# First block of a two-block transformer kernel: queries and keys move to chunks 2 to 4 of the projection, keys are turned first, VectorE turns a quarter of the queries

## The chip, the cores and the metric

The kernel runs on one core of one Trainium2 chip. The metric is the device time of one execution in microseconds (us), the median of several runs.

## The reference

The program computes two blocks on 512 tokens of width 1024. The change lies in the first block, whose part that matters is this:

```python
u  = rms_norm(h, norm_w) * (1 + scale) + shift        # 512 tokens
uc = rms_norm(hc, norm_w) * (1 + scale_c) + shift_c   # 256 context tokens
p = u @ w_in                       # q, k, v, a gate for attention, a | g for the convolution, a gate for it
q, k, v = qk_heads(p, ...)         # 8 query heads, 2 key heads of width 64, each rms-normed
q, k = rope_2d(q, angles), rope_2d(k, angles)
k_c, v_c = kv_heads(uc @ w_in[:, K_LO:V_HI], ...)
attn = softmax(q @ [k_c, k].T / 8) @ [v_c, v] * silu(p[za])     # 768 keys
conv = pointwise(silu(layer_norm(depthwise_conv_31(a * sigmoid(g))))) * silu(p[zc])
h = h + gate * (concat[attn, conv] @ w_out)
```

shift, scale and gate are rows of silu(c) @ w_mod, the "modulation". The second block has its own w_mod_2 (24 groups of 512 columns), and a mixer of two attentions: one of them ("dsa") scores 4 query tiles of 128 rows for each of 8 heads, tile q against (q + 1) * 128 keys.

## The kernel before, in words

**Chunks.** Every weight matrix is read in chunks of 256 columns. SyncE (SP) loads chunk n + 2 once VectorE is done with chunk n (`lo_done`). ScalarE (ACT) rounds it to a high part (`split_high`, L1372), VectorE (DVE) subtracts to get the low part (`split_low`, L1825), and TensorE (PE) multiplies three times, high by high, high by low and low by high. Chunk n uses the PSUM banks `acc` of its parity. In the first block the chunks are in this order: 0 to 3 are the convolution's g, a, g, a (`N_GLU`), 4 and 5 are queries (`N_Q`), 6 is keys and values with the context's (`N_KV`), 7 to 10 the two gates (`N_ZA`, `N_ZC`), 11 and 12 the pointwise product (`N_PW`), 13 to 16 the output (`N_WO`). Products of 0 to 3 and 7 on put channels on partitions (`product`, L843 to L845), those of 4 to 6 put tokens there (`by_token`, L863 to L866).

**The program of each engine** is a list in its own fixed order, and engines meet only at semaphores. The loop `for n in range(N_PW)` stands once in the program of PE, once in ACT's and once in DVE's.

**Modulation groups.** A group g of 512 modulation columns is read in 4 ticks (SP's `load_tick`) after the chunks `ticks_of(n)` names; chunk n carries half of group 4 + n // 2, and chunk 10 all four ticks of group 9. Up to `G_POOL` = 10 PE does the sums as small matmuls (`tick`, L775), ACT copies the row (`copy_group`), PE turns it (`turn_group`, L788) and DVE adds the bias (`group_columns`, L1837). From group 10 on GpSimd (POOL) sums them in place (`sum_tick`, L620, L623, L627), and PE adds the partitions (L782). PE's tick of an even chunk waits for `group_columns` of the group before it. Group columns stand in DVE's list in the middle of its taps.

**Queries and keys.** After chunk 6 ACT squares, DVE reduces, ACT takes the root (`qrs_rd`), DVE norms keys (`kn_rd`), and POOL norms the queries (L559, L561) and applies the rotation: for each of 4 token tiles first the keys (8 operations of 64 columns), then the queries (6 of 256), then it copies the context's keys (L586), and only then raises `rope_rd`. It then clears half of each key buffer (L594), since `kH`, `kL` (kept in the memory of `uH`, `uL`) hold each key head twice, padded with zeros to 128 partitions. PE, past chunk 10, waits for `rope_rd`, turns 4 query blocks (L897) and 2 key blocks (L900) through the banks `X` and `acc`; ACT rounds each (L1449, L1452, L1453) and DVE takes the low part (L1947, L1950, L1951).

**Taps.** The convolution is 124 taps (4 channel blocks of 31) on DVE, each 128x512 (L1883, L1885, L1887). Twelve (`TG`) stand in each of chunks 4 to 9, the rest lie in the attention's loop, five to three steps.

**Attention.** 32 steps (8 heads by 4 tiles). In each PE turns the exponentials (L928, 6 matmuls of 128), makes the scores of two steps ahead (L918 to L920, three of 512 and three of 256), and sums values (L939, 12 of 64). DVE takes maxima (L1958), ACT exponentiates (L1461) and moves (L1468).

**Second block.** In the dsa loop DVE's `dsa_max` (L2204) and `dsa_move` (L2211) take their width from the list `ROWS` = (3, 0, 2, 1), PE and ACT take theirs from i % 4.

Of the kernel before, what the change touches and what calls it, by code (L numbers as in the profile page):

```python
# [14 lines left out]
P = 128  # L15
# [13 lines left out]
G_POOL = 10  # L29
# [14 lines left out]
N_GLU, N_Q, N_KV, N_ZA, N_ZC, N_PW, N_WO = 0, 4, 6, 7, 9, 11, 13  # L44
# [18 lines left out]
U_LN = (36, 44, 52)  # L63

# [57 lines left out]
def program(nc, t, out):  # L122
    ctx = ExitStack()
    with ctx:
# [71 lines left out]
        ctx_read, sq_rd, qv_rd, qrs_rd, rope_rd = sem("ctx_read"), sem("sq_rd"), sem("qv_rd"), sem("qrs_rd"), sem("rope_rd")  # L196
        qkT, qk_hi, qk_lo, kz_rd = sem("qkT"), sem("qk_hi"), sem("qk_lo"), sem("kz_rd")
# [34 lines left out]
        def overlay(specs):  # L232
            with ExitStack() as o:
# [14 lines left out]
        gt, = overlay([("gt", [P, 4, 256], F32)])  # L248
# [4 lines left out]
        kH, kL = (w[:, :, :].rearrange("p k n -> p (k n)")[:, 0:3072].rearrange("p (e g n) -> p e g n", e=2, g=2)  # L253
                  for w in (uH, uL))
# [67 lines left out]
        for j in range(2):  # L322
            sources += [cut(w_in, glu + 512 + WCOL * j), cut(w_in, glu + WCOL * j)]
        sources += [cut(w_in, WCOL * j) for j in range(2)] + [cut(w_in, k_lo)]
# [77 lines left out]
        def key_banks(j):  # L402
            return X[:, 0:2, :].rearrange("p a n -> p (a n)")[:, 0:768] if j == 4 else pair[1][:, 0:768]
# [124 lines left out]
        def _(pool):  # L528
# [29 lines left out]
            for tt in range(TT):  # L558
                link(g.tensor_tensor(qv[:, tt], qv[:, tt],  # L559
                                     qrs[:, tt * NH:tt * NH + NH].unsqueeze(2).to_broadcast([P, NH, HD]), ALU.mult))  # L560
                link(g.tensor_tensor(qv[:, tt], qv[:, tt],  # L561
                                     qkw[:, 0:1, :].to_broadcast([P, NH, HD]), ALU.mult))
            pool.wait_ge(kn_rd, 1)
            for tt in range(TT):
                for heads, src, dsts in ((2, kvt[:, 2 + tt, 0:P], [0, 1]), (NH, qtok[:, tt], None)):
# [10 lines left out]
                    if dsts is None:  # L576
                        link(g.tensor_tensor(one, tm[0], tm[1], ALU.subtract))
                        link(g.tensor_tensor(two, tm[2], tm[3], ALU.add))
                    else:
                        for e in dsts:  # L580
# [3 lines left out]
            for c in range(CT):  # L584
                for e in range(2):
                    last = g.tensor_copy(kdup[:, c, :, e, :], kv[:, c])  # L586
                    if c < CT - 1 or e == 0:
                        link(last)
            last.then_inc(rope_rd, 1)
            pool.wait_ge(chunk_done, N_PW)  # L590
            pool.wait_ge(rope_rd, 1)
            for i in range(4):
                half = slice(HD, P) if i % 2 == 0 else slice(0, HD)
                g.memset((kH, kL)[i // 2][half, i % 2].bitcast(F32), 0.0).then_inc(kz_rd, 1)  # L594
                pool.wait_ge(kz_rd, i + 1)

# [40 lines left out]

            for g_ in range(G_POOL, G_DVE[0]):
                sum_ticks(g_, range(4))
# [108 lines left out]
        def _(pe):  # L748
# [76 lines left out]
            def product(n, a, nk, u0, xh, xl, w_hi, w_lo, turn=None, k0=0, first=True, done=True, ready=u_lo, near=None, ends=None):  # L825
# [8 lines left out]
                for i, (m, k) in enumerate(steps):  # L834
                    o = acc[:, 2 * (a % 2) + m, :]
                    if i == nk and turn is not None:
                        turn_group(turn)
                    if i == nk and near is not None:
# [30 lines left out]
            whi_v, wlo_v = wT[1], wT[2]  # L869
            for n in range(N_PW):  # L870
                turn = 3 + n // 2 if n and n % 2 == 0 else None
                if N_Q <= n < N_ZA:
# [7 lines left out]
                else:  # L880
                    product(n, n, KT, U_U if n == 0 else None, uH, uL, wT[1], wT[2], turn)
# [6 lines left out]
            pe.wait_ge(rope_rd, 1)  # L888
            pe.wait_ge(ctx_read, 1)
            for j in range(6):  # L890
                if j in (2, 3, 4):
                    pe.wait_ge(qk_lo, j if j == 4 else j - 1)
                if j == 5:
                    acc_gone(pe, N_PW - 2)
                if j < 4:
                    for tt in range(TT):
                        last = tr(X[:, j % 2, tt * P:tt * P + P], qtok[:, tt, j * P:j * P + P], ident[:])  # L897
                else:
                    for c in range(6):
                        last = tr(key_banks(j)[:, c * P:c * P + P],  # L900
                                  kdup[:, c, j - 4].rearrange("p e d -> p (e d)"), ident[:])
                last.then_inc(qkT, 1)

            pe.wait_ge(qk_lo, 6)
            pe.wait_ge(kz_rd, 4)
            acc_gone(pe, N_PW - 1)
            acc_gone(pe, N_PW - 2)

            def scores(i):
                h, qt = i // 4, i % 4  # L910
                if i >= 2:
                    pe.wait_ge(p_rd, i - 1)
                ql = slice(qt * P, qt * P + P)
# [9 lines left out]
            def turn(i):  # L923
                pe.wait_ge(p_rd, i + 1)
                if i >= 1:
# [5 lines left out]
            def values(i):  # L931
                h, qt = i // 4, i % 4
                o = X[:, 2, :] if h % 2 == 0 else modp[:, :]
                pe.wait_ge(pt_rd, i + 1)
                if qt == 0 and h >= 2:
# [8 lines left out]
            pe.wait_ge(mrow_rd, 10)  # L944
# [406 lines left out]
        def _(act):  # L1351
# [57 lines left out]

            for n in range(N_PW):  # L1410
                act.wait_ge(chunk_done, n + 1)
                if n in (0, 2):
# [1154 lines left out]
```

## Time and profile before

| what | value |
|---|---|
| median of 3 runs | 1951.15 us (1946.53 to 1953.48) |
| the profiled execution's own time | 1951.19 us |
| its span, first to last instruction | 1949.5 us |
| busy PE, DVE, ACT, POOL | 1723.2, 1026.1, 653.0, 591.1 us |

The profile is one execution. Its views used here are the timeline of an engine (start, duration, operation, in brackets the idle time before it and who ended it), the windows (busy time of each engine in a stretch and the granted clock of TensorE, where 1.00 is 2.4 GHz and 0.50 is 1.2 GHz), groups of instructions by line, and what one line did in a stretch. A merged row "x12" gives the time from the first start to the last end.

### The profile page before, as it was taken

The page shows a single profiled execution, that of the slowest core. Times are in us where ns is not written, and L with a number is a line of the kernel's source. Part 1 is how long each engine was busy: PE and PEld are TensorE (multiplying, and loading weights), DVE is VectorE, ACT ScalarE, POOL GpSimd, SP SyncE. Part 2 cuts the span into 40 slices and gives each one's busy share as a digit, 9 for nine tenths or more (in the row PEclk, how much of TensorE's full clock was granted, in tenths as well). Part 3 has the DMA queues.
Part 4 walks back from the last instruction along what each step waited for, and adds up shares of the span by engine and source line. Part 5 has one row for each costly group of instructions (what it writes and reads, how often), then busy time and mean ns, then how long its engine had stood idle before and what let it go on. Part 6 is the DMA issues. An engine that isn't in the chain of part 4 may idle for free.

```text
span 1949.5 us, 23737 instructions
## 1 busy us (share of the span) xinstructions
PE 1723.2 (88%) x9380; PEld 1429.6 (73%) x9385; DVE 1026.1 (53%) x1305; ACT 653.0 (33%) x889; POOL 591.1 (30%) x515
## 2 busy tenths in 40 slices
PE   4997599788787789869999999899987799999997
PEld 3796489568786668748888787677766678888875
DVE  1568567575467675583333324655675743233344
ACT  4312255412122325243232212343444343332222
POOL 0005800262774000467887701222431300000012
PEclk8998799899788889989999999899997999999999
DMA  8553300143532000225565522221110222323221
GB/s 278 164 172 98 119 1 1 34 156 116 165 109 84 25 1 1 65 87 172 182 194 180 168 84 83 84 87 44 65 44 23 65 86 91 102 86 102 94 85 43
DMA packets 152521, 187.14 MB, mean 96 GB/s; under 512 B 6893, under 2 KB 117845, under 8 KB 152436
## 3 DMA queue, kind: packets, MB, share of 16 engines
q1 hardware_dynamic: 152436, 185.96, 29.6%
q8 instruction: 58, 0.95, 0.2%
q14 instruction: 27, 0.22, 0.0%
HBM read 183.85 MB, written 2.10 MB: 95 GB/s over the span
## 4 chain that ended last, share of the span: by engine, by line
PE 58%; POOL 16%; DVE 12%; issue 7%; ACT 4%; DMA 2%; POOLq 0%; SPq 0%; another core or an unknown queue 0%; DVEq 0%; ACTq 0%
PE ps L843 6%; PE ps L844 6%; PE ps L845 6%; POOL msum L627 5%; POOL mraw L620 5%; PE ps L1200 4%; PE ps L1201 4%; PE ps L1202 4%; PE ps L939 2%; PE ps L1234 2%; PE ps L863 2%; PE ps L1236 2%; PE ps L1235 2%; PE ps L865 2%; PE ps L866 2%
## 5 line engine op out<-in xcount | busy, mean ns | idle before, releaser
L1200 PE MATMUL ps<-uH,whi 128*128 128x512 f32 x704 | 278.6, 396 | 25.7 <-DVE uL L1841 25.4
L1202 PE MATMUL ps<-uH,wlo 128*128 128x512 f32 x704 | 276.5, 393 | 0.0
L1201 PE MATMUL ps<-uL,whi 128*128 128x512 f32 x704 | 276.1, 392 | 0.0
L1825 DVE TENSOR_TENSOR wlo<-wraw,whi 128x2048 fp32r<-128x2048 f32 x64 | 157.3, 2458 | 178.6 <-ACT whi L1372 178.4
L620 POOL TENSOR_TENSOR mraw<-mraw,cpad 128x1024 f32<-128x1024 f32 x64 | 129.1, 2017 | 380.8 <-PE ps L782 237.2
L1372 ACT ACTIVATE whi<-wraw 128x2048 fp32r<-128x2048 f32 x71 | 135.7, 1911 | 301.0 <-PE ps L845 268.0
L1200 PEld LDWEIGHTS ps<-uH,whi 128*128 128x128 f32 x704 | 133.7, 190 | 57.0 <-issue 20.8
L2344 DVE TENSOR_TENSOR wlo<-wraw,whi 128x2048 fp32r<-128x2048 f32 x22 | 51.2, 2327 | 206.8 <-ACT whi L1677 206.8
L1202 PEld LDWEIGHTS ps<-uH,wlo 128*128 128x128 f32 x704 | 133.4, 190 | 28.5
L1201 PEld LDWEIGHTS ps<-uL,whi 128*128 128x128 f32 x704 | 133.8, 190 | 27.4
L627 POOL TENSOR_TENSOR msum<-msum,mraw 128x512 f32<-128x512 f32 x96 | 150.8, 1571 | 7.5
L843 PE MATMUL ps<-hH,whi 128*128 128x512 f32 x352 | 140.6, 399 | 0.0
L844 PE MATMUL ps<-hL,whi 128*128 128x512 f32 x352 | 139.5, 396 | 0.0
L845 PE MATMUL ps<-hH,wlo 128*128 128x512 f32 x352 | 139.5, 396 | 0.0
L681 POOL TENSOR_TENSOR sqd<-sqd 128x512 f32<-128x512 f32 x2 | 2.8, 1384 | 429.0 <-ACT sqd L1628 429.0
L843 PE MATMUL ps<-uH,whi 128*128 128x512 f32 x320 | 130.3, 407 | 2.6 <-DVE uL L2237 1.4
L844 PE MATMUL ps<-uL,whi 128*128 128x512 f32 x320 | 127.2, 398 | 0.0
L863 PE MATMUL ps<-whi,uH 128*128 128x256 f32 (+1 forms) x416 | 121.2, 291 | 6.6 <-DVE uL L1841 6.6
L845 PE MATMUL ps<-uH,wlo 128*128 128x512 f32 x320 | 126.7, 396 | 0.0
L865 PE MATMUL ps<-wlo,uH 128*128 128x256 f32 (+1 forms) x416 | 120.0, 289 | 0.0
L866 PE MATMUL ps<-whi,uL 128*128 128x256 f32 (+1 forms) x416 | 119.8, 288 | 0.0
L1885 DVE SCALAR_TENSOR_TENSOR cy<-utp,cols,cy 128x512 f32<-128x512 f32 x116 | 94.1, 811 | 2.8
(452 smaller groups left out, 3663.3 us busy)
## 6 DMA issues: line engine op xcount, KB each, us to landing
mraw<-in_w_mod_dram SPq DMA_DIRECT2D x104, 512.0 KB, 3.9
wraw<-in_w_gate_dram SPq DMA_DIRECT2D x22, 1024.0 KB, 5.3
wraw<-in_w_up_dram SPq DMA_DIRECT2D x22, 1024.0 KB, 5.5
wraw<-in_w_down_dram SPq DMA_DIRECT2D x16, 1024.0 KB, 5.0
wraw<-in_w_in_dram SPq DMA_DIRECT2D x11, 1024.0 KB, 5.5
wraw<-in_w_in_even_dram SPq DMA_DIRECT2D x9, 1024.0 KB, 6.6
mfirst<-in_w_mod_dram SPq DMA_DIRECT2D x16, 512.0 KB, 7.2
wraw<-in_w_in_odd_dram SPq DMA_DIRECT2D x16, 512.0 KB, 4.5
```

The lines of the kernel that those rows point to most:

```text
L620: g.tensor_tensor(w, w, cpad[:, 2 * kp:2 * kp + 2, 2:3].to_broadcast([P, 2, GW]), ALU.mult).then_inc(msum_rd, 1)
L627: g.tensor_tensor(msum[:], msum[:], w[:, kk], ALU.add).then_inc(msum_rd, 1)
L843: mm(o, h, xh[:, k0 + k], start=(first and k == 0), stop=False)
L844: mm(o, h, xl[:, k0 + k], start=False, stop=False)
L845: last = mm(o, l, xh[:, k0 + k], start=False, stop=(done and k == nk - 1))
L863: mm(oo, xh[:, k, xs], h, start=(k == 0 and (u0 is None or tt % 2 == 0)), stop=False, skip_group_check=u0 is not None)
L865: mm(oo, xh[:, k, xs], l, start=False, stop=False, skip_group_check=u0 is not None)
L866: last = mm(oo, xl[:, k, xs], h, start=False, stop=(k == KT - 1), skip_group_check=u0 is not None)
L1200: mm(o, h_, uH[:, k], start=(k == 0), stop=False)
L1201: mm(o, h_, uL[:, k], start=False, stop=False)
L1202: last = mm(o, l_, uH[:, k], start=False, stop=(k == KT - 1))
L1825: V.tensor_tensor(wlo[:, n % 2, :], wraw[:, n % 2, :], whi[:, n % 2, :].bitcast(F32), ALU.subtract).then_inc(lo_done, 1)
```

## The change

Chunks 2 to 4 of the projection are now queries and keys with values, chunks 5 and 6 the second half of g and a. POOL rotates the keys of all four tiles first, copies the context's, raises `rope_rd` to 1, and then rotates three of the four query tiles (`rope_rd` 2). DVE norms and rotates the fourth (`turn_query`, semaphore `rope_v`) after chunk 5's split. PE turns the keys in the middle of chunk 10 (`key_jobs`), ACT and DVE round them there; after chunk 10 PE turns the four query blocks into four separate banks. Keys have a buffer of their own without zero padding, and the scores contract over the 64 partitions of a head. The first score waits for the first query block alone. Group 9 of the modulation goes to POOL (`G_POOL` = 9), after `rope_v`. The taps are spread as `TAPS_AT` says (68 before the attention in place of 72, 56 in it), and chunk 12's split moves from chunk 10 to steps 2 and 3 of the attention. In the dsa loop DVE's widths are (i % 4 + 1) * 128.

```diff
-G_POOL = 10
+G_POOL = 9
-N_GLU, N_Q, N_KV, N_ZA, N_ZC, N_PW, N_WO = 0, 4, 6, 7, 9, 11, 13
+N_GLU, N_Q, N_KV, N_ZA, N_ZC, N_PW, N_WO = (0, 5), 2, 4, 7, 9, 11, 13
+TAPS_AT = {2: 8, 3: 10, 5: 9, 6: 9, 7: 12, 8: 12, 9: 8}
+ROPE_DVE = 3
-        gt, = overlay([("gt", [P, 4, 256], F32)])
+        gt, kH, kL = overlay([("gt", [P, 4, 256], F32), ("kH", [P, 2, 768], F32R), ("kL", [P, 2, 768], F32R)])
...
 # POOL
-            for tt in range(TT):
-                for heads, src, dsts in ((2, kvt[:, 2 + tt, 0:P], [0, 1]), (NH, qtok[:, tt], None)):
+            for heads in (2, NH):
+                for tt in range(TT):
+                    if heads == NH and tt == ROPE_DVE:
+                        continue
...
-            pool.wait_ge(chunk_done, N_PW)
-            pool.wait_ge(rope_rd, 1)
-            for i in range(4):
-                half = slice(HD, P) if i % 2 == 0 else slice(0, HD)
-                g.memset((kH, kL)[i // 2][half, i % 2].bitcast(F32), 0.0).then_inc(kz_rd, 1)
...
+            pool.wait_ge(rope_v, 1)
             for g_ in range(G_POOL, G_DVE[0]):
                 sum_ticks(g_, range(4))
...
 # PE
+            def key_jobs():
+                pe.wait_ge(rope_rd, 1)
+                pe.wait_ge(ctx_read, 1)
+                acc_gone(pe, N_PW - 2)
+                for j in range(2):
+                    for c in range(6):
+                        last = tr(key_banks(j)[:, c * P:c * P + P], kdup[:, c, j].rearrange("p e d -> p (e d)"), ident[:])
+                    last.then_inc(qkT, 1)
+
+            def query_jobs():
+                pe.wait_ge(rope_rd, 2)
+                pe.wait_ge(rope_v, 1)
+                pe.wait_ge(qk_lo, 1)
+                pe.wait_ge(mod_rd, G_POOL)
+                for j in range(4):
+                    for tt in range(TT):
+                        last = tr(oTp[j][:, tt * P:tt * P + P], qtok[:, tt, j * P:j * P + P], ident[:])
+                    last.then_inc(qkT, 1)
...
 # PE, scores
-                    q_h, q_l = qH[:, h // 2, ql], qL[:, h // 2, ql]
-                    k_h, k_l = kH[:, h % 2, h // 4, c0:c1], kL[:, h % 2, h // 4, c0:c1]
+                    q_h, q_l = qH[half, h // 2, ql], qL[half, h // 2, ql]
+                    k_h, k_l = kH[half, h // 4, c0:c1], kL[half, h // 4, c0:c1]
...
 # DVE
+            def turn_query(tt):
+                v = qtok[:, tt].rearrange("p (h d) -> p h d", d=HD)
+                dve.wait_ge(u_lo, U_UC + 8)
+                link(V.tensor_tensor(v, v, qrs[...], ALU.mult))
+                link(V.tensor_tensor(v, v, qkw[...], ALU.mult))
...
+                V.tensor_tensor(tm[0], one, cs, ALU.mult)
+                V.tensor_tensor(tm[1], two, sn, ALU.mult)
+                V.tensor_tensor(tm[2], one, sn, ALU.mult)
+                link(V.tensor_tensor(tm[3], two, cs, ALU.mult))
+                V.tensor_tensor(one, tm[0], tm[1], ALU.subtract)
+                V.tensor_tensor(two, tm[2], tm[3], ALU.add).then_inc(rope_v, 1)
...
+                if i == 3:
+                    split_low(N_PW + 1)
+                    continue
-                for _ in range(2 if i % 3 < 2 else 1):
+                for _ in range(1 if i % 6 == 5 else 2):
...
             def dsa_max(i):
-                w = (ROWS[i % 4] + 1) * P
+                w = (i % 4 + 1) * P
...
             def dsa_move(i):
-                w = (ROWS[i % 4] + 1) * P
+                w = (i % 4 + 1) * P
```

## Rows read from the trace of the kernel before

**Rows 1.** Windows: stretch, busy of each engine (instructions), TensorE clock, DMA share, GB/s

```profile
234.00:247.00 13.00, 6.63 (x29) 5.34 (x28) 6.58 (x8) 6.89 (x9) 5.38 (x4) 0.50 0.00 1
...
262.00:342.00 80.00, 80.00 (x644) 76.41 (x642) 60.08 (x86) 44.83 (x79) 0.00 (x0) 1.00 0.00 1
```

**Rows 2.** Timeline of TensorE: chunk 0, then from chunk 1's tick to attention

```profile
60.35 0.39 PE L843 MATMUL ps<-uH,whi 128*128 128x512 f32 x1
...
61.03 0.39 PE L843 MATMUL ps<-uH,whi 128*128 128x512 f32 x1
...
81.36 1.08 PE L775 MATMUL ps<-mraw,cpad 128*32 128x128 f32 x32
...
107.27 1.08 PE L775 MATMUL ps<-mraw,cpad 128*32 128x128 f32 x32
...
132.80 1.08 PE L775 MATMUL ps<-mraw,cpad 128*32 128x128 f32 x32
...
151.29 1.08 PE L775 MATMUL ps<-mraw,cpad 128*32 128x128 f32 x32
...
163.45 1.08 PE L775 MATMUL ps<-mraw,cpad 128*32 128x128 f32 x32
...
186.85 1.93 PE L775 MATMUL ps<-mraw,cpad 128*32 128x128 f32 x32 [11.08 <-DVE mod L1837]
...
233.82 1.97 PE L897 MATMUL ps<-ident,qtok 128*128 128x128 f32 x8 [12.08 <-POOL kdup L586]
...
246.95 0.80 PE L918 MATMUL ps<-uH,qH 128*128 128x512 f32 x1 [4.34 <-DVE uL L1951]
...
251.31 1.19 PE L928 MATMUL ps<-ident,ptb 128*128 128x128 f32 x6 [0.15 <-ACT ptb L1461]
```

**Rows 3.** Timeline of VectorE, 107 to 244 us

```profile
107.43 1.23 DVE L1898 TENSOR_TENSOR utp<-ps,sgt 128x1024 f32<-128x1024 f32 x1 [4.68 <-PE ps L845]
...
151.47 0.69 DVE L1907 COPY kvt<-ps 128x512 f32<-128x512 f32 x1 [4.45 <-PE ps L866]
...
218.66 2.70 DVE L1825 TENSOR_TENSOR wlo<-wraw,whi 128x2048 fp32r<-128x2048 f32 x1
...
243.02 0.95 DVE L1950 TENSOR_TENSOR uL<-ps,uH 64x768 fp32r<-64x768 f32 x1 [3.29 <-ACT uH L1453]
```

**Rows 4.** Timeline of GpSimd, 163 to 234 us

```profile
163.95 1.59 POOL L559 TENSOR_TENSOR qtok<-qtok,small 128x512 f32<-128x512 f32 x1 [159.09 <-ACT small L1433]
...
185.98 0.71 POOL L582 TENSOR_TENSOR kdup<-gt 128x64 f32<-128x64 f32 x1
...
192.25 2.67 POOL L577 TENSOR_TENSOR qtok<-gt 128x256 f32<-128x256 f32 x1
195.00 1.07 POOL L578 TENSOR_TENSOR qtok<-gt 128x256 f32<-128x256 f32 x1
...
227.60 0.73 POOL L572 TENSOR_TENSOR gt<-qtok,ropet 128x256 f32<-128x256 f32 x1
```

**Rows 5.** Timeline of ScalarE: the table load ahead of the root

```profile
161.00 1.28 ACT L1433 ACT_TABLE_LOAD   x1 [4.17 <-DVE small L1916]
```

**Rows 6.** The taps' line, 163.9 to 176.5 us: ns minimum/median/maximum

```profile
L1885 DVE SCALAR_TENSOR_TENSOR cy<-utp,cols,cy x6: 752/1418/1670, 163.9 to 173.9; 128x512 f32<-128x512 f32 x6
```

**Rows 7.** Groups by line and form, 247 to 347 us: busy us, mean ns

```profile
L1885 DVE SCALAR_TENSOR_TENSOR cy<-utp,cols,cy 128x512 f32<-128x512 f32 x49 | 36.6, 747 | 0.7
L1958 DVE TENSOR_REDUCE small<-ps 128x1 f32<-128x768 f32 x32 | 30.6, 957 | 25.7 <-PE ps L920 25.5
```

**Rows 8.** Timeline of TensorE: the partition sums of group 10, in chunk 14

```profile
402.32 1.87 PE L782 MATMUL ps<-small,msum 128*128 128x1 f32 x8 [3.54 <-POOL msum L627]
```

**Rows 9.** Timeline of GpSimd: group 10, an operation of each kind

```profile
378.07 1.90 POOL L620 TENSOR_TENSOR mraw<-mraw,cpad 128x1024 f32<-128x1024 f32 x1 [138.52 <-PE ps L788]
...
406.34 1.28 POOL L623 TENSOR_TENSOR msum<-mraw 128x512 f32<-128x512 f32 x1
```

**Rows 10.** Windows: the dsa loop of the second block, columns as in rows 1

```profile
727.00:778.00 51.00, 48.71 (x380) 43.33 (x385) 30.37 (x67) 26.04 (x82) 0.00 (x0) 1.00 0.01 1
```

More of the change, by code:

```diff
@@ L575, in _ @@
                     link(g.tensor_tensor(tm[3], two, cs, ALU.mult))
-                    if dsts is None:
+                    if heads == NH:
                         link(g.tensor_tensor(one, tm[0], tm[1], ALU.subtract))
-                        link(g.tensor_tensor(two, tm[2], tm[3], ALU.add))
+                        last = g.tensor_tensor(two, tm[2], tm[3], ALU.add)
+                        if tt == max(x for x in range(TT) if x != ROPE_DVE):
+                            last.then_inc(rope_rd, 1)
+                            pool.wait_ge(rope_rd, 2)
+                        else:
+                            link(last)
                     else:
-                        for e in dsts:
+                        for e in range(2):
                             d = kdup[:, 2 + tt, :, e, :].rearrange("p h (a z f) -> p h a z f", a=2, z=2)
@@ L823, in _, with product @@
                 input_tile(f)
-            def product(n, a, nk, u0, xh, xl, w_hi, w_lo, turn=None, k0=0, first=True, done=True, ready=u_lo, near=None, ends=None):
+            def product(n, a, nk, u0, xh, xl, w_hi, w_lo, turn=None, k0=0, first=True, done=True, ready=u_lo, near=None, ends=None, mid=None):
                 pe.wait_ge(lo_done, n + 1)
@@ L837, in product @@
                         turn_group(turn)
+                    if i == nk and mid is not None:
+                        mid()
                     if i == nk and near is not None:
@@ L880, in _ @@
                 else:
-                    product(n, n, KT, U_U if n == 0 else None, uH, uL, wT[1], wT[2], turn)
+                    product(n, n, KT, U_U if n == 0 else None, uH, uL, wT[1], wT[2], turn, mid=key_jobs if n == N_PW - 1 else None)
                 for f in CTX_TILES.get(n, ()):
@@ L934, in values @@
                 pe.wait_ge(pt_rd, i + 1)
+                if qt == 0 and h < 2:
+                    pe.wait_ge(qk_lo, 5 + h)
                 if qt == 0 and h >= 2:
@@ L1408, in _, with key_high @@
             split_high(1)
+            def key_high(j):
+                act.wait_ge(qkT, j + 1)
+                src = key_banks(j)
+                A(kH[:, j], src, ACT.Copy).then_inc(qk_hi, 1)
             for n in range(N_PW):
+                if n == N_PW - 1:
+                    for j in range(2):
+                        key_high(j)
                 act.wait_ge(chunk_done, n + 1)
-                if n in (0, 2):
-                    if n == 2:
-                        acc_gone(act, 1)
+                if n in N_GLU:
+                    if n == N_GLU[1]:
+                        acc_gone(act, N_GLU[0] + 1)
                     A(sgt[:], acc[:, 2 * (n % 2):2 * (n % 2) + 2, :], ACT.Sigmoid).then_inc(acc_read[n % 2], 2)
```

134 lines of the change are left out of this document (65 added, 69 removed).

## The prediction

> **What bounds the kernel now.** I read the page's busy shares first: TensorE is busy most of the span, so a change in the first block is worth what TensorE stands still there. The windows of that block come next. Between the projection and the attention lie 12 us in which TensorE does nothing and GpSimd works [rows 2, 4], then 13 us at clock 0.50 with TensorE half busy and nobody full [rows 1]. The attention behind them is full: 80.00 us busy of 80, clock 1.00. The timeline of TensorE says who ends each gap [rows 2]: 11.08 us at 186.85 (a tick waits for group columns that stand behind VectorE's taps), 12.08 us at 233.82 (GpSimd's last copy for keys). From 233.82 to 246.95 each block is turned, rounded and subtracted, and the scores wait for the last key low part. VectorE has no gap of note from 151.47 until its last split ends at 221.36 [rows 3]. So there are two limits in turn: up to 221 VectorE, then GpSimd's rotation, begun only at 163.95 because keys are chunk 6 [rows 4], then a serial 13 us.
>
> My measuring point is the first turn of exponentials, at 251.31 [rows 2]: from there on the attention has its regular step.
>
> **Chunks 2 to 4.** Two convolution chunks with their ticks take 107.27 - 81.36 = 25.9 us, two query chunks 132.80 - 107.27 = 25.5 us, the key chunk 151.29 - 132.80 = 18.5 us [rows 2]. In the new order the key chunk ends at 81.36 + 25.5 + 18.5 plus about 1.4 us for the turn and the context's tiles that lay beside the old chunk 2: 126.8 us, 24.5 us earlier. The loads keep their sequence by position and their gates, so SP is not later.
>
> **GpSimd.** The root comes as late after the key chunk as now: table load at 161.00, done 162.3 [rows 5], 11 us after 151.29; so GpSimd starts near 138. Of its work at the present rates beside a busy VectorE: 6 norms at about 1.55 (9.3 us), 32 key operations at 0.79 start to start (25.3), 4 copies at 0.8 (3.2), 18 query operations at 1.15 (20.7), and for each of four 2048-wide splits that it meets about 1.6 more, as the row at 192.25 has 2.67 where its neighbour has 1.07 [rows 4] (6.4). Sum 65: keys ready near 178, queries near 203. A full tile with VectorE idle takes 0.73 an operation, so this errs to the late side.
>
> **TensorE** from 126.8: six products at 151.29 to 163.45 = 12.2 each [rows 2] are 73, plus some 4 us at the tick that waits for group columns (11.08 now; the taps before it are 7 of 12, and VectorE is ahead of where it was), plus 2 for 12 key transposes (8 of the query's took 1.97 at half clock): end near 205. Group 9's matmuls and their wait for loads are gone. The key transposes stand mid-chunk 10, and behind them wait ACT's copies and its gate, all with room.
>
> **VectorE** is therefore last. From 151.47 to 221.36 [rows 3] it did 69.9 us: copy, five splits, the reductions, 48 taps, the key norm. From 126.9 the same work ends at 196.8. Added: one more split (2.7), 2 taps (1.5), the a by g product (1.23 [rows 3]), `turn_query`, which no row shows (two multiplies of 512 and six of 256; nearest is the tap at 0.75 for 512 [rows 7], so between 8 x 0.4 = 3.2 and 8 x 0.75 = 6.0; I take 4.8, as six are half as wide and GpSimd interferes), the wait for the root that taps fill today (1.5), and GpSimd's interference, which now covers all of VectorE's stretch and the start of group 9 (3; between 0 and 6). Sum 14.7: taps end near 211.5. The low part of two keys follows, 0.95 each [rows 3]; the first frees the X banks at 212.5.
>
> **The serial part.** First query block: 4 transposes 1.0 (8 took 1.97 at half clock [rows 2]), copy and low part 0.7 each, as VectorE's copy of 512 columns [rows 3], in all 2.5 us with hand-overs; the scores start near 215 in place of 246.95, and the turn 4.3 us after as now: 219.3. Saved: 251.3 - 219.3 = 32 us. Both ends: 27 with interference and `turn_query` at the upper bounds, 38 if both are at the lower and the clock is not down.
>
> **Group 9 on GpSimd.** It runs beside the attention's first eight steps, 4 operations of 1.90 and 7 of 1.28 [rows 9]: 16.6 us alone. Beside GpSimd's 512-wide operations a tap took a median of 1.42 and up to 1.67 us against 0.75 [rows 6, 7], so about 0.8 us of VectorE for 512 columns, 1.6 for 1024: 12 us, of which some 2 are in the 3 above. A step lasts 2.98 us (24 matmuls; 80 us for 644 [rows 1]) and VectorE needs 0.96 + 1.83 x 0.75 + 0.1 = 2.4 of it. Eight steps spare 4.5, the slack between a step's maxima and its turn is about 1.3 by my estimate (one more step's work, 3, less maxima and exponentials); the split at step 3 in place of two taps costs 0.9. Give-back 10 + 0.9 - 5.8 = about 5; I take 4, because GpSimd waits for loads between ticks. Bounds 0 and 8. SP stands behind these ticks with chunk 13, needed only after the attention.
> By the Trainium skill (SBUF — State Buffer, two separate sides) the port pair of GpSimd and VectorE is an exclusive lock held for the whole instruction, which would be all 16.6 us and a give-back near 9. The norms do not look like that: taps and GpSimd's 1.4 to 1.6 us operations alternate at about 1.55, not at 2.1.
>
> **Chunk 12's turn.** Group 9 is now added over partitions (8 matmuls, 1.87 [rows 8], in place of one transpose of some 0.4); GpSimd's group 10 starts on that turn at 378.07 [rows 9], and TensorE waits for that group at 402.32: +1.5 us, bounds 0 and 4.
>
> **At nothing.** The memsets lie beside the serial part. Four fewer taps before and four more in the attention: covered by the 0.6 us a step; without that cover 3 us. ACT's split at step 2: it is busy 44.83 of 80 us there [rows 1], so 2 us are made up in two steps. The dsa widths: TensorE is busy 48.71 of 51 us there [rows 10], so at most 2.3 us gained; the new width is larger for two of four tiles, 0 to +1. I take 0. The 64-partition scores: columns streamed are the same; no row of this kernel has such matmuls. Nearest are the ticks, which use 32 of the array's columns: a product of 48 matmuls at 0.227 (three in 0.68 us [rows 2]) is 10.9, its tick 1.08, together 12.0 of 12.16, so at most 0.1 for each change of shape. That is 0.2 us a step, 0 to 6.4 in all; I take 0, as a change of operation stands there already.
> The Trainium skill (TensorEngine Tiling (Array Packing), Key Properties) says that changing the tiling mode drains the array; this speaks against the change, and each step would change twice. No row here prices it.
>
> **Sum.** -32 + 4 + 1.5 = -26.5 on the profiled execution's 1951.19, which is the median of 1951.15 within 0.1: 1924.5, so 1925 us. All later stages shift.
>
> **Rivals.**
> (a) The gain stays whole: VectorE keeps up in the attention, interference small: -31 to -38, 1913 to 1920. For it: the step's slack and the load pauses. Against: taps at 1.42.
> (b) The rotation or VectorE is later than I count, a plain shift of the same limit. If each GpSimd query operation takes 1.55 as a norm does, its queries are ready at 210; ten more us of delay make it last: gain 15 to 20, 1931 to 1936. For it: rows at 2.67. Against: start at 138 and 8 us of room.
> (c) The 64-partition scores cost 0.2 us a step: 1931.
> (d) Slower than before: the same scores cost much more. The gain of 26.5 is spent at 0.83 us for each of 32 steps. At clock 0.50 the scores of two steps took 4.3 us (246.95 to 251.31 [rows 2]); if half-filled operands held TensorE at that level through the attention, a step would go from 2.98 to about 5.4 and the time to 2000. For it: nothing seen. Against: the fill at 1.00 with 64-column values.
> (e) The change does not do what it says: VectorE's list is the limit whatever the order, because its 70 us only move. It decides if VectorE had no idle time to fill before 151; but it had 4.45 and 4.68 us gaps and more [rows 3]. Then the 12 and 13 us are saved only in part: 1945 to 1952.
>
> **How the numbers follow.** My forecast 0.48, (a) 0.17, (b) 0.16, (c) 0.09, (d) 0.04, (e) 0.06. This kernel's times can be told apart from about 0.3% (5.9 us). Faster: all but (d) and half of (e), rounded 0.92; same 0.04; slower 0.04. The range 1910 to 1939 takes in (a), (b) and (c) and leaves out (d), (e).
>
> **What would show it.** Right: keys' copy on GpSimd ends near 178, queries near 203; the gap before the query transposes is under 8 us and ended by VectorE, not by GpSimd; the first turn of exponentials at 216 to 223; TensorE's idle time in the attention is ended by VectorE maxima in its first eight steps only; step still 2.98 afterwards. Wrong: a step longer throughout (c, d), GpSimd as releaser of the transposes (b), VectorE's taps ending past 220 (e), or a gap at chunks 11 to 14 that grew by more than 4 us because group 10 or chunk 13's load came late.

## The result, and the profile after

| | median (range), runs | ratio to before, 95% interval |
|---|---|---|
| before, on the same chip | 1950.91 us (1946.53 to 1953.48), 4 | |
| after | 2030.47 us (2026.59 to 2034.34), 4 | 1.0405 [1.0383, 1.0426] |

The change makes the kernel 4.1% slower; I had forecast 1925 us, and rival (d), the one on the other side, is what happened. The span grew from 1949.5 to 2026.5 us, by 77.0. Three stretches give it: up to the first turn of exponentials 17.6 us were won (233.71 against 251.31), from there to the first matmul of the convolution's mean 194.9 us passed in place of 95.2 (428.6 against 346.5 at the end), and 5.1 us came back behind it. -17.6 + 99.7 - 5.1 = 77.0.

The windows of the kernel after, with the columns of [rows 1] (busy time of PE, PEld, DVE, ACT, POOL with instructions, the clock, the DMA share, GB/s):

```profile
107.00:127.00 20.00, 20.00 (x192) 19.67 (x192) 17.22 (x24) 2.98 (x4) 0.00 (x0) 1.00 0.47 158
127.00:205.00 78.00, 75.75 (x524) 62.05 (x523) 67.77 (x75) 24.74 (x23) 57.41 (x61) 1.00 0.41 135
205.00:223.00 18.00, 4.42 (x20) 3.31 (x18) 17.75 (x11) 1.02 (x1) 17.29 (x10) 0.73 0.35 117
223.00:236.00 13.00, 8.21 (x36) 7.01 (x37) 8.92 (x10) 6.37 (x10) 1.89 (x2) 0.63 0.00 0
236.00:262.00 26.00, 26.00 (x99) 22.16 (x99) 12.30 (x14) 9.98 (x16) 0.00 (x0) 0.50 0.16 54
262.00:430.00 168.00, 168.00 (x653) 146.08 (x654) 61.93 (x90) 46.65 (x77) 0.00 (x0) 0.50 0.01 5
```

In the attention TensorE is busy 168.00 us of 168, as it was busy 80.00 of 80 before [rows 1], and yet the clock is 0.50 and not 1.00. 653 matmuls take 168 us where 644 took 80. VectorE is busy 37% of that stretch and ScalarE 28%: nothing makes TensorE wait, it runs at 1.2 GHz. The timeline of TensorE shows the moment:

```profile
226.77 3.61 PE L899 MATMUL ps<-ident,qtok 128*128 128x128 f32 x16 [17.34 <-DVE kL L1936]
230.30 0.50 PE L935 MATMUL ps<-kH,qH 64*128 64x512 f32 x1
230.64 0.40 PE L936 MATMUL ps<-kL,qH 64*128 64x512 f32 x1
...
233.71 1.54 PE L947 MATMUL ps<-ident,ptb 128*128 128x128 f32 x6 [1.03 <-ACT ptb L1482]
235.18 0.79 PE L935 MATMUL ps<-kH,qH 64*128 64x512 f32 x1
235.77 0.62 PE L936 MATMUL ps<-kL,qH 64*128 64x512 f32 x1
```

The lines at 226.77, 230.30 and 233.71 stand for the rows at 233.82, 246.95 and 251.31 in [rows 2]. The stop ahead of the query transposes is now ended by VectorE, as I had said, but it is 17.34 us and not under 8. The first scores at 230.64 run at full speed (0.40 us for 512 columns), so the clock had risen by the end of the transposes. Behind a stop of 1.03 us the turn at 233.71 is slow, the same score matmul takes 0.62 us at 235.77, and it stays so for 195 us: a step is 6.25 us in place of 2.98.

Why the first turn came at 233.7 and not at 219.3 stands in the timelines of VectorE and, in the second fence, of GpSimd:

```profile
191.69 15.57 DVE L1908 SCALAR_TENSOR_TENSOR cy<-utp,cols,cy 128x512 f32<-128x512 f32 x12
207.30 3.87 DVE L1848 TENSOR_TENSOR wlo<-wraw,whi 128x2048 fp32r<-128x2048 f32 x1
211.09 1.74 DVE L1908 SCALAR_TENSOR_TENSOR cy<-utp,cols,cy 128x512 f32<-128x512 f32 x1
...
219.99 5.52 DVE L1908 SCALAR_TENSOR_TENSOR cy<-utp,cols,cy 128x512 f32<-128x512 f32 x3
225.55 1.82 DVE L1936 TENSOR_TENSOR kL<-ps,kH 128x768 fp32r<-128x768 f32 x2
```

```profile
202.80 2.21 POOL L629 TENSOR_TENSOR mraw<-mraw,cpad 128x1024 f32<-128x1024 f32 x1
...
209.10 4.86 POOL L636 TENSOR_TENSOR msum<-msum,mraw 128x512 f32<-128x512 f32 x2
...
221.71 3.26 POOL L636 TENSOR_TENSOR msum<-msum,mraw 128x512 f32<-128x512 f32 x2
```

GpSimd's queries are ready at 202.7, and group 9 follows at once, until 224.97. Beside it a split takes 3.87 us, against 2.70 in [rows 3], and a tap 1.63 to 2.19 (median 1.63), against 0.75 in [rows 7]. VectorE ends its last tap with GpSimd, not 8.5 us behind the queries.

### The profile page after: what moved, and what is told of

It is laid out like the page before. It is cut to its first block, busy times and chain, and to the rows that moved or that the text cites. A ratio compares the mean times of both kernels' runs of the same rounds, so it can differ in the third digit from the quotient of the medians.

```text
span 2026.5 us, 23639 instructions
## 1 busy us (share of the span) xinstructions
PE 1812.9 (89%) x9328; PEld 1499.4 (74%) x9328; DVE 1041.2 (51%) x1311; ACT 656.1 (32%) x887; POOL 599.5 (30%) x514
## 4 chain that ended last, share of the span: by engine, by line
PE 59%; DVE 15%; POOL 12%; issue 7%; ACT 4%; DMA 2%; POOLq 0%; SPq 0%; DVEq 0%; ACTq 0%
PE ps L855 6%; PE ps L857 6%; PE ps L856 6%; POOL msum L636 5%; PE ps L960 4%; POOL mraw L629 4%; PE ps L1220 4%; PE ps L1222 4%; PE ps L1221 4%; PE ps L947 2%; PE ps L1254 2%; PE ps L1256 2%; PE ps L1255 2%; DVE cy L1908 2%; PE ps L875 2%
## 5 line engine op out<-in xcount | busy, mean ns | idle before, releaser
L629 POOL TENSOR_TENSOR mraw<-mraw,cpad 128x1024 f32<-128x1024 f32 x68 | 135.7, 1996 | 477.2 <-PE ps L792 471.8
L636 POOL TENSOR_TENSOR msum<-msum,mraw 128x512 f32<-128x512 f32 x102 | 163.6, 1604 | 8.0
L1908 DVE SCALAR_TENSOR_TENSOR cy<-utp,cols,cy 128x512 f32<-128x512 f32 x116 | 101.6, 876 | 2.8
```

Source lines behind the costliest of these rows:

```text
L629: g.tensor_tensor(w, w, cpad[:, 2 * kp:2 * kp + 2, 2:3].to_broadcast([P, 2, GW]), ALU.mult).then_inc(msum_rd, 1)
L636: g.tensor_tensor(msum[:], msum[:], w[:, kk], ALU.add).then_inc(msum_rd, 1)
L1908: link(V.scalar_tensor_tensor(cy[:, j], utp[:, j, k:k + SEQ], w, cy[:, j], ALU.mult, ALU.add))
```

## The experiments

The kernels of one group ran on one chip with the kernel before beside them (medians of 7 runs: 1953.17 us for e1 to e4, 1953.74 for e5 to e8, 1950.47 for e9 to e12). Ratios are to these. "Attention" is the time from the first turn of exponentials to the first matmul of the mean, in the profiled execution.

| label | median, runs | ratio [95%] | first turn | attention | clock in it |
|---|---|---|---|---|---|
| e1_before_half | 2054.04, 4 | 1.0502 [1.0483, 1.0522] | 251.2 | 194.9 | 0.50 |
| e2_after_full | 1928.84, 4 | 0.9871 [0.9854, 0.9887] | 233.9 | 94.0 | 1.00 |
| e3_after_mix | 1931.69, 1 | | 232.8 | 100.2 | 1.00 |
| e4_after_pad | 1933.47, 4 | 0.9898 [0.9881, 0.9914] | 236.6 | 95.6 | 1.00 |
| e5_first4 | 1942.31, 1 | | 233.1 | 104.9 | 1.00 |
| e6_last16 | 1977.94, 2 | 1.0128 [1.0096, 1.0160] | 234.6 | 139.9 | 0.50, then 1.00 |
| e7_busy | 2031.47, 4 | | 232.0 | 194.1 | 0.50 |
| e8_pad_late | 1924.64, 4 | 0.9853 [0.9826, 0.9881] | 221.9 | 98.0 | 1.00 |
| e9_busy_start | 1941.27, 4 | 0.9946 [0.9928, 0.9964] | 232.6 | 105.5 | 1.00 |
| e10_late_turn | 1922.21, 4 | 0.9846 [0.9820, 0.9873] | 219.3 | 98.5 | 1.00 |
| e11_keys_alone | 1924.48, 4 | 0.9865 [0.9844, 0.9886] | 224.8 | 97.6 | 1.00 |
| e12_both | 1921.34, 4 | 0.9853 [0.9835, 0.9870] | 220.8 | 97.3 | 1.00 |

First turns compare to about 2 us only: the profiled executions already differ at the tick of chunk 1, ahead of chunk 2, the first that the change moves (81.36 us before, 82.97 after, 80.79 in e8, 83.36 in e6). Counted from that tick the kernel after wins 19.2 us up to its first turn, and not 17.6.

### Do the 64-partition scores alone do it?

**e1_before_half**: the kernel before, with nothing but the scores over the 64 partitions of a head (its keys are kept twice, so the result is the same).

```diff
-                    q_h, q_l = qH[:, h // 2, ql], qL[:, h // 2, ql]
-                    k_h, k_l = kH[:, h % 2, h // 4, c0:c1], kL[:, h % 2, h // 4, c0:c1]
+                    q_h, q_l = qH[half, h // 2, ql], qL[half, h // 2, ql]
+                    k_h, k_l = kH[half, h % 2, h // 4, c0:c1], kL[half, h % 2, h // 4, c0:c1]
```

> The kernel before with one edit: the score matmuls contract over the 64 partitions of a head (the zero half of the key buffer is left out of the operands); everything else as before. Theory T1 (score matmuls on 64 partitions hold TensorE at clock 0.50 for the whole attention): the stretch from the first turn of exponentials to the end of the attention goes from 95 us to about 32 x 6.25 = 200 us, clock 0.50 in it, total 1951 + 100 to 105 = 2050 to 2056. Rival T2 (the clock is low because of how the attention is entered, after 17 us of idle TensorE; 64 partitions are neutral): 1948 to 1954, step 2.98, clock 1.00. Rival T3 (each change of shape costs time at full clock): step 3.0 to 3.4, total 1951 to 1965, clock 1.00.

**e2_after_full**: the reverse, the kernel after with scores over all 128 partitions (it then sums the products of two heads).

```diff
-                ql, half = slice(qt * P, qt * P + P), slice(HD * (h % 2), HD * (h % 2) + HD)
+                ql, half = slice(qt * P, qt * P + P), slice(0, P)
```

> The changed kernel with one edit: the score matmuls read all 128 partitions of queries and keys, so that each score is the sum over the two heads of a block; this part of the computation is changed, its instructions and sizes are otherwise those of the kernel before. T1: the step falls from 6.25 to about 3.0, clock 1.00, total 2030 - 103 = 1925 to 1932. T2: clock stays 0.50 because the entry is the same, total 2025 to 2035. T3: step 3.0 but the gain only 32 x 0.2 = 6 us, total near 2022.

**e4_after_pad**: the kernel after, with each query block rounded twice, once for each head of its pair with the other head's partitions multiplied by zero, so that the scores run over 128 partitions and the result is that of the reference. ScalarE and VectorE each do four more operations ahead of the attention.

```diff
-                    q_h, q_l = qH[half, h // 2, ql], qL[half, h // 2, ql]
+                    q_h, q_l = (qH, uH)[h % 2][:, h // 2, ql], (qL, uL)[h % 2][:, h // 2, ql]
...
-                A(qH[:, j], oTp[j], ACT.Copy).then_inc(qk_hi, 1)
+                A(qH[:, j], oTp[j], ACT.Copy, scale=masks[0])
+                A(uH[:, j], oTp[j], ACT.Copy, scale=masks[1]).then_inc(qk_hi, 1)
```

> The changed kernel with queries padded to 128 partitions: ScalarE and VectorE write each turned query block twice, once times a column that is 1 on the lower and 0 on the upper 64 partitions and once the other way round (the second copy in the memory of uH and uL, free by then); keys keep their unpadded buffer, which holds the same head in both halves. The scores are the reference's. T1: as e2, plus four copies and four subtractions in the serial part (about 2 to 3 us, 0.60 and 0.69 each, partly beside each other): 1928 to 1936, faster than the kernel before by about 15 to 22 us. T2: 2025 to 2035.

Windows of e1:

```profile
247.00:262.00 15.00, 14.85 (x52) 12.26 (x53) 6.74 (x8) 5.37 (x10) 0.00 (x0) 0.50 0.00 0
262.00:342.00 80.00, 80.00 (x309) 68.92 (x307) 28.27 (x40) 23.44 (x39) 0.00 (x0) 0.50 0.00 1
```

The same stretch of 262 to 342 us in which the kernel before did 644 matmuls at 1.00 [rows 1] holds 309 at 0.50. The one edit costs 5.0%, and its reversal in e2 gives the change back a gain of 1.3%: from the same start (first turn at 233.9 against 233.7) the attention takes 94.0 us in place of 194.9. With padded queries and the reference's result the change is worth 1.0%. So the rest of the change, taken together, wins; the operand's height is the loss.

### Do they lower the clock, or keep it from rising?

**e3_after_mix** has 128 partitions in steps 0 to 15 and 64 in 16 to 31, **e5_first4** 128 in the first four steps only, **e6_last16** 64 in steps 0 to 15 and 128 behind them. Each step with 128 sums two heads' products. One line differs:

```diff
+ (slice(0, P) if i < 16 else slice(HD * (h % 2), HD * (h % 2) + HD))     # e3
+ (slice(0, P) if i < 4 else slice(HD * (h % 2), HD * (h % 2) + HD))      # e5
+ (slice(0, P) if i >= 16 else slice(HD * (h % 2), HD * (h % 2) + HD))    # e6
```

> The changed kernel with 128-partition scores in steps 0 to 15 (each score there is the sum over two heads, which changes that part of the computation) and 64-partition scores in steps 16 to 31. T1: clock 1.00 and step 3.0 in the first 16 steps, then clock 0.50 and step 6.25 from within a few steps of the switch; total near 1930 + 52 = 1980. T2: one clock level for the whole attention, total near 1930 or near 2030.

> The changed kernel with scores over all 128 partitions in the first 4 of the 32 steps (one head, all query tiles) and over 64 partitions in the other 28. It changes what is computed: in those 4 steps the sum of two heads' products stands for one head's. Theory A (the level on entry decides: 64-partition scores don't lower a clock of 1.00, but keep one of 0.50 from rising): the clock rises in the first 4 steps and then stays 1.00, steps of about 3.39 us from the fifth on, attention some 94 + 28 x 0.41 = 105 us, total about 1940. Theory B (64-partition scores pull the clock down, only more slowly than the mixed kernel of 16 and 16 let them show): the clock falls back to 0.50 some tens of microseconds after the fifth step, total 1960 to 2015.

> The mirror: scores over 64 partitions in steps 0 to 15, over 128 in steps 16 to 31 (which then compute the sum of two heads' products). Theory A: 16 steps of 6.25 us at clock 0.50, then the clock rises within a few steps and the rest run at 2.98: 100 + 6 x 1 + 48, about 153 us from the first turn to the mean against 195, total 1983 to 1990. Theory B (once the clock has been low in this phase, something else, such as the steps' own waits, holds it there): the clock stays 0.50 to the end of the phase, total above 2020.

Windows of e5, the stretch behind its four steps of 128 partitions:

```profile
262.00:335.00 73.00, 73.00 (x524) 63.69 (x523) 51.56 (x75) 39.19 (x66) 0.00 (x0) 1.00 0.00 1
```

Windows of e6, around step 16:

```profile
310.00:320.00 10.00, 10.00 (x43) 8.93 (x42) 5.25 (x8) 2.79 (x5) 0.00 (x0) 0.50 0.01 2
320.00:330.00 10.00, 10.00 (x68) 9.45 (x66) 5.16 (x7) 4.31 (x7) 0.00 (x0) 0.82 0.00 0
330.00:340.00 10.00, 10.00 (x84) 9.61 (x83) 7.84 (x13) 5.82 (x10) 0.00 (x0) 1.00 0.01 2
```

The theory that scores over 64 partitions simply hold TensorE at 0.50 fell here. In e3 and e5 the same steps follow full ones and the clock is 1.00 to the end, for 16 and for 28 steps. In e6 they come first, and the clock stands at 0.50 from the first turn on through the steps of 64; the first scores over 128 partitions are those of step 16, issued two steps ahead at 320.38, and the turn at 324.31 is at full speed again. Once they run steadily, such steps keep the level that they find, either one. (e3 and e5 are one execution each. e5 had a second one, of 2281 us at a mean clock of 0.715 over its whole span, more than the attention at 0.50 can add; the level of its attention is not known, and it speaks for neither side.)

### What sets the level at the start?

**e7_busy** is the kernel after, all scores over 64 partitions, with 140 matmuls that nobody reads in TensorE's long stop. **e9_busy_start** has ten more in the short stop between the first scores and the first turn. Neither changes what the kernel computes.

```diff
+            def keep_busy(count, o=X[:, 2, 0:256]):
+                for _ in range(count):
+                    mm(o, uH[:, 0, 0:P], uH[:, 0, 0:256], start=True, stop=True)
...
             def query_jobs():
+                keep_busy(140)
                 pe.wait_ge(rope_rd, 2)
...
             scores(0)
             scores(1)
+            pe.wait_ge(qk_lo, 4)                   # e9 alone
+            keep_busy(10, X[:, 1, 0:256])          # e9 alone
             for i in range(NS):
```

> The changed kernel as it is (all scores over 64 partitions), with 140 matmuls of 256 columns over 128 partitions, whose results nobody reads, in the 17 us in which TensorE waits for the keys' low parts ahead of the query transposes. Theory A: TensorE enters the attention at clock 1.00 and stays there, steps of 3.39 us, 32 x 3.39 = 108 at most against 195 from the first turn to the mean; total about 2030 - 87 to - 95, so 1935 to 1944. Theory B (64-partition scores hold the clock low whatever the engine did before): clock 0.50 from about 240 on, total above 2015. Rival C (the clock holds in part: enters at 1.00 and falls somewhere within the phase): in between, and the place of the fall is read from the windows.

> The changed kernel with all scores over 64 partitions, 140 matmuls of 256 columns over 128 partitions ahead of the query transposes as in the kernel before this one, and 10 more between the first two steps' scores and the first turn of the exponentials, where TensorE stood still for 1.26 us when the clock fell. Theory A (the phase has two stable levels, and the start decides: two steps' scores over 64 partitions and the stop behind them let the clock fall, the later steps don't): the clock stays 1.00 in all or nearly all executions, attention about 100 us, total 1936 to 1942. Theory B (the steps themselves sit at the edge and the clock falls sooner or later in most executions): most executions at 1960 to 2035, with the fall somewhere after 240.

Windows of e7, and in the second fence of e9:

```profile
223.00:230.00 7.00, 6.02 (x46) 5.41 (x45) 6.24 (x9) 3.06 (x5) 1.46 (x1) 1.00 0.00 0
230.00:236.00 6.00, 4.74 (x23) 3.75 (x21) 2.83 (x5) 3.04 (x7) 0.00 (x0) 0.75 0.00 0
236.00:262.00 26.00, 26.00 (x100) 22.20 (x99) 11.56 (x13) 10.42 (x16) 0.00 (x0) 0.50 0.24 81
```

```profile
223.00:230.00 7.00, 6.03 (x48) 5.51 (x47) 6.25 (x7) 2.41 (x5) 2.03 (x2) 1.00 0.00 0
230.00:236.00 6.00, 6.00 (x39) 4.99 (x38) 3.63 (x6) 3.85 (x7) 0.00 (x0) 1.00 0.00 0
262.00:335.00 73.00, 73.00 (x524) 63.70 (x523) 51.57 (x75) 39.28 (x66) 0.00 (x0) 1.00 0.00 1
```

e7 missed its number, and says more than a hit would have: a clock of 1.00 up to the attention didn't help. Behind two steps' scores and a stop of 1.26 us the first turn, at 231.98, is still at full speed (0.87 us), and the score matmul behind it, at 232.78, is not (0.62). Three of its four executions took 2031 to 2035 us. The fourth took 1938.12 at a mean clock of 0.949. With ten matmuls in that stop all four executions of e9 are at 1938 to 1944. So it is the start of the attention that lets the clock go, and the later steps keep what they find. That the ten matmuls did it is likely and not proven: e7 and e9 ran on different chips, with three low executions of four against none of four.

The kernel after, e1 and e7 start with half-height scores and a stop or a cold engine. e2, with full height, comes out of the same start at full speed (first row below, where the kernel after has 1.54). e4, whose first turn follows a longer stop of 3.27 us, does fall to 0.50, and is back at 1.00 within 4 us (its windows in the second fence):

```profile
233.85 0.87 PE L947 MATMUL ps<-ident,ptb 128*128 128x128 f32 x6 [1.12 <-ACT ptb L1482]
```

```profile
238.00:241.00 3.00, 3.00 (x13) 2.79 (x12) 2.07 (x3) 1.44 (x4) 0.00 (x0) 0.50 0.00 0
242.00:262.00 20.00, 20.00 (x162) 19.16 (x162) 16.63 (x21) 12.94 (x22) 0.00 (x0) 1.00 0.30 107
```

Full height brings the clock back, half height doesn't. What of it the clock answers to, the idle half of the rows or the time lost at the two changes of height in each step (next section), no run separates.

### What do they cost at full clock?

One step in e2 (128 partitions), and in the second fence in e9 (64 partitions), both at 1.00:

```profile
244.73 0.82 PE L947 MATMUL ps<-ident,ptb 128*128 128x128 f32 x6
245.31 0.47 PE L935 MATMUL ps<-kH,qH 128*128 128x512 f32 x1
...
246.32 0.28 PE L937 MATMUL ps<-kH,qL 128*128 128x256 f32 x1
246.44 1.45 PE L960 MATMUL ps<-kvt,ptT 128*128 128x64 f32 x12
247.72 0.82 PE L947 MATMUL ps<-ident,ptb 128*128 128x128 f32 x6
```

```profile
241.49 0.83 PE L952 MATMUL ps<-ident,ptb 128*128 128x128 f32 x6
242.25 0.49 PE L940 MATMUL ps<-kH,qH 64*128 64x512 f32 x1
...
243.28 0.28 PE L942 MATMUL ps<-kH,qL 64*128 64x256 f32 x1
243.49 1.55 PE L965 MATMUL ps<-kvt,ptT 128*128 128x64 f32 x12
244.88 0.83 PE L952 MATMUL ps<-ident,ptb 128*128 128x128 f32 x6
```

A matmul of 256 columns takes 0.28 us at either height: the columns cost the same, as I had said. But from the turn to the first score 0.76 us pass in place of 0.58, from the last score to the values 0.21 in place of 0.12, and from the values to the next turn 1.39 in place of 1.28. The step is 3.39 against 2.99: 0.40 us, of which 0.18 and 0.09 lie at the two changes of height, 0.11 between values and turn and 0.02 within the scores. Over the attention it is 105.5 against 94.0, 11.5 us.

The Trainium skill (TensorEngine Tiling (Array Packing), Key Properties) says that changing the tiling mode drains the array. These rows agree in kind.

### Where did the front's other 14 us go?

**e8_pad_late** adds to e4 one wait, so that group 9 starts behind the first scores. **e10_late_turn** adds to e8 a later turn of group 4 in chunk 2, ahead of which TensorE stood 3.47 us for ScalarE's copy. **e11_keys_alone** adds to e8 that GpSimd's norms of the queries wait for VectorE's of the keys. **e12_both** has both.

```diff
             pool.wait_ge(rope_v, 1)
+            pool.wait_ge(s_rd, 1)                                       # e8, e10 to e12
...
-                    if i == KT and turn is not None:
+                    if i == (2 if n == 2 else 1) * KT and turn is not None:   # e10, e12
...
+            pool.wait_ge(kn_rd, 1)                                      # e11, e12: moved up from behind the loop
             for tt in range(TT):
                 if tt == ROPE_DVE:
                     continue
```

> The changed kernel with zero-padded queries (scores over 128 partitions, same result) and GpSimd's sums of group 9 held back until the first scores are done, so that nothing of GpSimd runs beside VectorE's last taps ahead of the attention. Theory: those taps (8 in 14.4 us after group 9's start) go back to about 1.0 to 1.3 us each, the keys' low parts end 4 to 5 us earlier, and the first turn comes at about 231 to 232 against 236.6; the sums of groups 9 to 11 move beside the attention, where they cost 0 to 2 us. Total 1927 to 1931 against 1933.5. Rival: VectorE has as much to do and what ends the wait is the same, or the sums beside the attention slow its maxima by as much: 1933 to 1936.

> The kernel with padded queries and GpSimd's group 9 behind the first scores, and in chunk 2 the transpose of group 4's sums behind two token tiles instead of one, so that TensorE doesn't stand 3.47 us at 84.9 for ScalarE's copy of these sums. Theory: chunks 2 to 4 end 2.5 to 5 us earlier (the last copy of keys at about 126 to 128 against 130.4), VectorE's and GpSimd's lists start that much earlier, and as VectorE idles under 1 us from 140 to 211, the first turn comes 2 to 4 us earlier; total 1920 to 1923 against 1924.6. Rival: the loads of the chunks' weights or ScalarE end the wait anyway, no change.

> The kernel with padded queries and GpSimd's group 9 behind the first scores, and GpSimd starting the queries' norms only when VectorE's 12 norms of the keys are done. Theory (GpSimd's work beside VectorE costs VectorE time): the 12 norms take 2.6 to 3.2 us against 8.4, VectorE's list ends 4 to 5 us earlier, but GpSimd starts some 3 us later than before, its queries are turned at about 203 instead of 200.6, still ahead of chunk 10's end; first turn at 217 to 219 against 221.9, total 1920 to 1922. Rival: TensorE's chunks, which end at about 209, bound the front, and only 1 to 2 us are gained.

> Both of these edits together: if both act on VectorE's list, first turn at 214 to 217 and total 1916 to 1920; if TensorE's chunks bound the front, total 1920 to 1922.

VectorE's timeline in e8, the same items as in the kernel after:

```profile
189.57 13.13 DVE L1914 SCALAR_TENSOR_TENSOR cy<-utp,cols,cy 128x512 f32<-128x512 f32 x12
202.74 2.29 DVE L1854 TENSOR_TENSOR wlo<-wraw,whi 128x2048 fp32r<-128x2048 f32 x1
204.95 0.74 DVE L1914 SCALAR_TENSOR_TENSOR cy<-utp,cols,cy 128x512 f32<-128x512 f32 x1
...
208.62 2.32 DVE L1914 SCALAR_TENSOR_TENSOR cy<-utp,cols,cy 128x512 f32<-128x512 f32 x3
210.97 1.82 DVE L1942 TENSOR_TENSOR kL<-ps,kH 128x768 fp32r<-128x768 f32 x2
```

Without group 9 beside it the twelve taps take 13.13 us and not 15.57, the split 2.29 and not 3.87, and the last eight taps with the group's columns 6.0 (204.95 to 210.97) and not 14.4 (211.09 to 225.5). That is 12.5 us, and with a start 2.1 us earlier (80.79 against 82.93 at the tick of chunk 1, so none of the edit's doing) the first turn moves from 236.6 in e4 to 221.9. e4's own rows for these items are those of the kernel after to within 0.01 us. The attention, which group 9 now lies beside, takes 98.0 us and not 95.6. The ratios of e4 and e8 differ by 0.0045, 8.8 us, less than the 14.7 - 2.4 = 12.3 of the two profiles up to the mean, of which 2.1 are the earlier start. Their spans differ by 9.7, so 2.6 us were lost behind the mean: there e8 has TensorE wait 3.04 and 5.41 us for VectorE's splits, at 355.40 and 397.40, where e4 has one such wait, of 1.38, and e4's wait of 3.54 for GpSimd's group 10 is gone.

e10's copy of the keys starts at 127.8 against 130.4 and its first turn at 219.3 against 221.9, as expected. Its execution reached the tick of chunk 1 later, at 82.44, so the edit gave 4.3 us up to the keys; in the time its ratio can't be told from e8's. e11's theory was right in its first half and wrong in its sum. VectorE's timeline:

```profile
143.51 1.30 DVE L1981 TENSOR_TENSOR kvt<-kvt,msum 128x128 f32<-128x128 f32 x6
148.70 3.36 DVE L1854 TENSOR_TENSOR wlo<-wraw,whi 128x2048 fp32r<-128x2048 f32 x1 [3.89 <-ACT whi L1397]
151.98 1.53 DVE L1922 TENSOR_TENSOR qtok<-qtok,small 128x512 f32<-128x512 f32 x1
```

The twelve norms of keys took 2.6 us and not 8.4, but VectorE then stood still 3.89 us for ScalarE's high part, and the split and the query's rotation now met GpSimd's norms (3.36 us against 2.28 and 1.53 against 0.81). The interference moved; it didn't go. e12 has the lowest median, 1921.34, but e8, e10, e11 and e12 are one result within their intervals: 1.4 to 1.5% faster than before.

## Why the prediction was wrong, by its own steps

**The step that failed** is "The 64-partition scores", which I put among the edits "at nothing", as "columns streamed are the same". The columns do cost the same; two other things don't. In the kernel after this edit costs 194.9 - 94.0 = 100.9 us. 11.5 of them are the change of shape at full clock, and the remaining 89.4 the clock: 194.9 against e9's 105.5. The term that I had sized between 0 and 6.4 us was outside its bounds even at full clock: I took the price of a change, at most 0.1 us, from a chunk product and its tick, which change the columns in use (128*32) and not the height, and a change of height cost about 0.2.

**Rival (d)** had the place, the clock and nearly the size, with 5.4 us a step forecast and 6.25 measured, 2000 us forecast and 2030 measured. It did not have that the same scores also run at 1.00 (e3, e5, e9). I gave it 0.04. Against it I set "the fill at 1.00 with 64-column values", and that was the wrong evidence: values of 64 columns use all 128 partitions of the operands, so they say nothing of a height of 64. No row of before could have settled it. A cost with no row, in the middle of the one phase that TensorE fills, repeated 32 times, deserved more than 0.04, and my range should have reached it.

By the Trainium skill (TensorE: Matmul & The Clock Gate, Part 1) the clock follows how busy the engine has been. The windows don't show that alone: busy 168.00 us of 168 at 0.50 here, 63.00 of 63 at 1.00 in e2, with height as the one difference, and 73.00 of 73 at 1.00 in e9, at the same height.

**The front, -32**, became -17.6. Its steps, forecast and measured:

| step | forecast | measured |
|---|---|---|
| key chunk ends | 126.8 | 132.5 |
| GpSimd starts | 138 | 142.5 |
| keys, queries ready | 178, 203 | 180.4, 202.7 |
| TensorE ends chunk 10 | 205 | 209.4 |
| VectorE's taps end | 211.5 | 225.5 |
| first turn | 219.3 | 233.7 |

The key chunk was 5.7 us late. 1.6 of that stand already at the tick of chunk 1; most of the rest is the turn of group 4, which I counted as work and not as a wait. In the kernel after:

```profile
90.60 0.47 PE L798 MATMUL ps<-ident,msum 128*128 128x128 f32 x1 [3.48 <-ACT msum L1400]
```

In e10, without that wait, tick to keys takes 45.4 us, as forecast. GpSimd made up its lateness, as its work took 60.2 us and not 65. What failed is the term for VectorE's interference, "and the start of group 9 (3; between 0 and 6)". My own steps had the queries ready at 203 and the last tap at 211.5, so group 9 had at least 8.5 us beside VectorE, and the overlap prolonged itself as both engines slowed (its operations take 16.6 us alone): in the end all 22.2 us of group 9 lay ahead of the attention. I had worked out 12 us for VectorE beside the whole group, and the measured figure is 12.5, but I booked 2 of them here and the rest, as **"Group 9", +4**, beside the attention. There the kernel after had nothing to give back; e8, which puts the group there, gives back 2.4 us, within the bounds of 0 to 8. **Rival (b)**, a front late by a plain shift and a gain of 15 to 20, has the front's 17.6 in its range, by VectorE's lateness and not by GpSimd's rates: most query operations took 1.07 us there, not 1.55.

By the Trainium skill (SBUF — State Buffer, two separate sides) VectorE would be locked out for all of GpSimd's instruction. The rows come near that and stay below it: in 22.2 us GpSimd did what takes 16.6 alone and VectorE what takes 22.2 - 12.5 = 9.7, together 26.3, so some 4 us ran side by side.

**Chunk 12's turn, +1.5**, was nothing: the wait that I had put at risk is 3.55 us after and 3.54 in [rows 8]. The 5.1 us that came back behind the mean appear behind that wait, in the next chunks; e4 has 3.4 of them and e9 none, and the executions of one kernel spread by 5 to 10 us, so I name no cause. **The dsa widths** at nothing held: from the first to the last start of the maxima it is 49.6 us after and 49.0 before. **Rival (e)** was half right: its sign, taps ending past 220, did come (225.5), and VectorE's list ends the stop ahead of the query transposes in every version of the new front; in e8 its waits from 140 to 211 add up to 0.55 us. But the front was won by 17.6 us all the same.

## What to carry to other kernels

Before an operand's height is cut in a phase that TensorE fills, look at what the clock does ahead of that phase, and try the cut alone: here filling the other 64 partitions with zeros cost 8 short operations ahead of the phase, 2.9 us, and brought the kernel from 2030 to 1933 us. When work is moved to GpSimd, take its start from your own timetable and count every microsecond until VectorE's next deadline as shared, with the prolongation that sharing brings. If a stop ahead of a filled phase can't be avoided, a row of matmuls that nobody reads can hold the clock through it (1941 us against 2030 here), and here it held in all executions only when it also covered the short stop behind the first results.

## What the runs showed of the hardware

**Two levels for one phase.** Steps with scores over 64 partitions, transposes and values over 128, ran at 0.50 through whole phases of 195 us with TensorE never idle, and at 1.00 through 16, 28 and 32 steps, with the same instructions. The level that the first steps left decided; being at 1.00 during the first scores was not enough (after, e6, e7). The same kernel (e7) took 2031 to 2035 us three times and 1938 once.

**Level and height.** From 0.50 the clock rose within 4 us of the first scores over 128 partitions (e6, 320.38 to 324.31) and some 5 us in the kernel before (from 246.95), and never in up to 32 steps over 64 (after, e1, e6, e7).

**A change of height** between matmuls cost about 0.2 us each at full clock, 0.40 us a step for two.

**VectorE beside GpSimd**: a tap of 512 columns with all operands in memory took 1.63 to 2.19 us beside GpSimd's sums and 0.75 alone, a norm of 128 columns 0.70 beside its norms (12 in 8.4 us) and 0.22 alone.
